# A decoder trunk on one core: where the dense pieces of a round stand, and how early casts and preparation are issued

## What is computed

```python
def reference(x, positions, ...):
    for i in range(DEPTH):
        p = x @ w_in                                   # attention, gate and r, k, v columns
        y_a = dsa_sparse_mqa(...)                      # top-64 keys of 256 for each query
        y_b = rwkv7_time_mix(pr, pk, v, pw, pa, pg, ...)
        g_a, g_b = jnp.split(jax.nn.sigmoid(p_gate + b_gate[i]), 2, axis=-1)
        x = layer_norm(alpha * x + (g_a * y_a + g_b * y_b) @ w_out[i], ...)
        x = layer_norm(alpha * x + conv_glu_ffn(x, w_up[i], ...), ...)

def step(state, inp):                                  # the recurrence, 16 heads of 64
    sa = jnp.einsum('bhvk,bhk->bhv', state, -kk_t)
    state = state * w_t[:, :, None, :] + sa[..., None] * b_t[:, :, None, :] \
            + v_t[..., None] * k_t[:, :, None, :]
    return state, jnp.einsum('bhvk,bhk->bhv', state, r_t)
```

## Time and profile before

| | us |
|---|---|
| median of 3 runs | 1269.19 (1268.2 to 1271.25) |
| the profiled execution's own time | 1277.04 |
| its span, first to last instruction | 1274.8 |
| PE busy in the span | 1160.5 (91%) |
| DVE busy | 785.9 (62%) |
| ACT busy | 537.2 (42%) |
| prologue and rounds, layer 0 (from the end of the scores to the last round's y) | 79.5 to 375.2 |
| the same, layer 1 | 712.1 to 1008.6 |

### The profile page before, as it was taken

One profiled execution on the slowest core, in us unless ns is written; L12 is line 12 of the kernel. 1 busy time (PEld: TensorE's weight loads), 2 busy tenths in 40 slices (PEclk: granted clock), 3 DMA queues, 4 the chain that ended last, 5 costly groups with the idle time before them and its releaser, 6 DMA issues.

```text
span 1274.8 us, 29251 instructions
## 1 busy us (share of the span) xinstructions
PE 1160.5 (91%) x12328; PEld 1042.2 (82%) x12328; DVE 785.9 (62%) x1436; ACT 537.2 (42%) x938; POOL 50.6 (4%) x56
## 2 busy tenths in 40 slices
PE   7996989898988899999999969898989898999997
PEld 7775878787878799998797758787878887999985
DVE  1338557675747777775522565667667577777745
ACT  2232445453534455654212424344545434556531
POOL 0000000000000100000000000000000001000000
PEclk9988999999999899999999978999999998999999
DMA  7422222222336365556464212212222464555561
GB/s 268 147 74 79 68 76 69 76 68 75 102 116 207 118 220 182 183 188 205 144 201 149 81 44 68 77 66 76 68 68 102 144 209 149 194 182 182 187 208 68
DMA packets 45353, 165.38 MB, mean 130 GB/s; under 512 B 5136, under 2 KB 5392, under 8 KB 44976
## 3 DMA queue, kind: packets, MB, share of 16 engines
q1 hardware_dynamic: 42576, 154.02, 36.3%
q0 software_dynamic: 1504, 7.47, 1.8%
q10 hardware_dynamic: 1152, 2.10, 0.5%
HBM read 160.42 MB, written 3.15 MB: 128 GB/s over the span
## 4 chain that ended last, share of the span: by engine, by line
PE 76%; DVE 17%; ACT 3%; issue 3%; DMA 1%; POOL 0%; DVEq 0%; SPq 0%; ACTq 0%
PE ps L722 18%; PE ps L723 16%; PE ps L724 16%; PE ps L869 8%; PE ps L697 5%; PE ps L1028 3%; DVE ring_r L1516 3%; DVE keep L1934 1%; PE ps L1070 1%; PE ps L881 1%; DVE small L1932 1%; PE ps L798 1%; PE ps L770 1%; ACT mid_hi L1192 1%; DMA ring<-stream_dram 1%
## 5 line engine op out<-in xcount | busy, mean ns | idle before, releaser
L722 PE MATMUL ps<-x_tok_r,mid_hi 128*128 128x256 f32 x448 | 138.6, 309 | 15.0 <-DVE ring_r L1516 15.0
L723 PE MATMUL ps<-xT_r,mid_hi 128*128 128x256 f32 x448 | 127.6, 285 | 0.0
L724 PE MATMUL ps<-x_tok_r,ring_r 128*128 128x256 f32 x448 | 127.4, 284 | 0.0
L722 PEld LDWEIGHTS ps<-x_tok_r,mid_hi 128*128 128x128 f32 x448 | 86.2, 192 | 25.3 <-issue 12.6
L697 PE MATMUL ps<-xT,ring 128*128 128x256 f32 x448 | 102.8, 388 | 0.0
L697 PEld LDWEIGHTS ps<-xT,ring 128*128 128x128 f32 x448 | 86.3, 195 | 13.8 <-issue 1.6
L1516 DVE TENSOR_TENSOR ring_r<-ring,mid_hi 128x1024 fp32r<-128x1024 f32 x64 | 77.9, 1219 | 25.0 <-ACT mid_hi L1192 25.0
L723 PEld LDWEIGHTS ps<-xT_r,mid_hi 128*128 128x128 f32 x448 | 86.7, 193 | 0.0
L724 PEld LDWEIGHTS ps<-x_tok_r,ring_r 128*128 128x128 f32 x448 | 86.5, 193 | 0.0
L1633 DVE COPY_PREDICATED X_Y<-masks,ps 128x256 f32<-128x256 uint32 x80 | 35.3, 441 | 66.0 <-PE ps L869 54.7
L1192 ACT CAST mid_hi<-ring 128x1024 fp32r<-128x1024 f32 x64 | 67.2, 1054 | 12.7 <-PE ps L724 12.7
(11 more groups left out here) (443 smaller groups left out, 3394.8 us busy)
## 6 DMA issues: line engine op xcount, KB each, us to landing
ring<-stream_dram SPq DMA_DIRECT2D x281, 512.0 KB, 3.4
lora_w<-lora_dram POOLq DMA_DIRECT2D x2, 1536.0 KB, 7.2
W_bt<-rpar_dram POOLq DMA_DIRECT2D x4, 512.0 KB, 4.5
kt_V<-rpar_dram POOLq DMA_DIRECT2D x4, 512.0 KB, 5.4
x_tok<-x_dram SPq DMA_DIRECT2D x2, 512.0 KB, 4.6
v_saved_dram<-vs_dC ACTq DMA_DIRECT2D x4, 256.0 KB, 3.9
x_tok<-x_dram SPq DMA_DIRECT2D x1, 1024.0 KB, 5.3
vf<-v_saved_dram ACTq DMA_DIRECT2D x4, 256.0 KB, 3.6
```

Of the source, the lines that this page charges most:

```text
L722: pe.matmul(dst, lh, rh, start=start, stop=False)
L723: pe.matmul(dst, lh, rl, start=False, stop=False)
L724: return pe.matmul(dst, ll, rh, start=False, stop=stop)
```

## The change

Every round still has its 16 pieces, and every task stays. What changes:

- **Gaps of the pieces.** Six in the levels, at gaps without a task: 0, 1, 5, 6, 9, 10 (first round: 5, 6, 7, 9, 10, 12). Ten in the chunk steps, which now have three gaps each, `fill(14 + 3c)` before Q, `15 + 3c` after Q and `16 + 3c` after y: all of 14 to 24 but 16.
- **Order of the pairs.** k, then r, then v, then the gates (`RKV_ORDER`); r ends in chunk step 0, v in chunk step 2. In the last round two gate pairs come before the two `oa` pairs.
- **Tasks.** The squares go from gap 13 to gap 12; `prep_rnx` from before Q1 to after y0.
- **ACT.** The cast of a chunk step stands ahead of the wait for Q, with a second call after it in steps 1 and 2; `resetY` is ahead of the wait for v.
- **DVE.** `att_norm` goes from the end of level 3 to ahead of it; the addition `Sa = S + own` (`chunk_t`) goes right behind Z; the subtractions follow the new casts; `prep_bk` goes from step 3 to step 2, ahead of `prep_v`.
- **Prologue.** On PE `prep_1` comes first, then two pieces, then `prep_ss` and `prep_v`; on DVE `prep_decay` and `prep_pend` come before `prep_ss`.

```diff
-LEVEL_GAPS = [list(range(4, 12))] + [[0, 1] + list(range(4, 10))] * (GROUPS - 1)
+LEVEL_GAPS = [[5, 6, 7, 9, 10, 12]] + [[0, 1, 5, 6, 9, 10]] * (GROUPS - 1)
+CHUNK_GAPS = [14, 15, 17, 18, 19, 20, 21, 22, 23, 24]
 OA_EARLY = 2
-GAPS = 14 + CHUNK_GAPS
+RKV_ORDER = (1, 0, 2)
+GAPS = 14 + 3 * NCH
...
+def gap_of(g, piece):
+    return (LEVEL_GAPS[g] + CHUNK_GAPS)[piece]
...
+def round_pairs(g):
     if g + 1 == GROUPS:
-        return [("oa", i) for i in range(OA_EARLY)]
-    return [("rkv", 3 * (g + 1) + 2)] + gates_of(g)
+        return gates_of(g) + [("oa", i) for i in range(OA_EARLY)]
+    return [("rkv", 3 * (g + 1) + t) for t in RKV_ORDER] + gates_of(g)
...
@@ PE, wkv @@
-                    fill(14 + 2 * c)
-                    if g + 1 < GROUPS and c == 1:
-                        prep_rnx(r + 1)
+                    fill(14 + 3 * c)
...
-                    fill(15 + 2 * c)
+                    fill(15 + 3 * c)
...
                     mm.then_inc(*pe_wkv.inc(r, f"y{c}"))
+                    if g + 1 < GROUPS and c == 0:
+                        prep_rnx(r + 1)
+                    fill(16 + 3 * c)
...
@@ PE, prologue @@
-                for k, p in enumerate((prep_ss, prep_1, prep_v, prep_rnT)):
-                    p(r0)
+                for k, ps_ in enumerate(([prep_1], [prep_ss, prep_v], [prep_rnT], [prep_rnx])):
+                    for p in ps_:
+                        p(r0)
                     for piece in first[2 * k:2 * k + 2]:
                         piece()
-                prep_rnx(r0)
...
                     if g + 1 < GROUPS:
-                        gaps[VALUES].append(lambda: prep_ss(r0 + g + 1))
+                        gaps[SQUARES].append(lambda: prep_ss(r0 + g + 1))
...
@@ ACT @@
             def chunk(r, c):
+                mids_up_to(r // GROUPS, mids_by(GAPS * (r % GROUPS) + 13 + 3 * c))
                 act.wait_ge(*pe_wkv(r, f"Q{c}"))
                 act.copy(Qs[:, :, :], step64(3)).then_inc(*act_wkv.inc(r, f"Q{c}"))
...
                         chunk(r, c)
-                        mids_up_to(l, mids_by(GAPS * g + 14 + 2 * c))
...
+                        if c in (1, 2):
+                            mids_up_to(l, mids_by(GAPS * g + 15 + 3 * c))
...
@@ DVE @@
-                prep_ss(r0)
                 prep_decay(r0)
                 prep_pend(r0)
+                prep_ss(r0)
                 topk(0)
...
                 prep_arc(r0)
+                prep_bk(r0)
                 prep_v(r0)
-                prep_bk(r0)
...
                     for lev in range(LEVELS):
+                        if lev == 3:
+                            att_norm(l, g)
                         if lev:
                             level(r, lev)
...
-                        if lev == 3:
-                            att_norm(l, g)
...
                             chunk_z(r, c)
+                            if c < NCH - 1:
+                                chunk_t(r, c)
+                            mids_up_to(l, mids_by(GAPS * g + 13 + 3 * c))
...
                             elif nxt and c == 2:
                                 prep_arc(r + 1)
+                                prep_bk(r + 1)
                             elif nxt:
                                 prep_v(r + 1)
-                                prep_bk(r + 1)
+                        else:
+                            mids_up_to(l, mids_by(GAPS * g + 13))
                         if c < NCH - 1:
                             chunk_s(r, c)
+                        if c in (1, 2):
+                            mids_up_to(l, mids_by(GAPS * g + 15 + 3 * c))
...
-                        mids_up_to(l, mids_by(GAPS * g + 13 + 2 * c))
```

More of the change, by code:

```diff
@@ L117, in gates_of, with pairs_done @@
     return [("gate", i) for i in range(start, start + GATES_CHUNKS[g])]
-def level_pairs(g):
-    return [("rkv", 3 * (g + 1)), ("rkv", 3 * (g + 1) + 1)] if g + 1 < GROUPS else gates_of(g)
-def chunk_gap(g, piece):
-    return piece * CHUNK_GAPS // max(4 * len(chunk_pairs(g)), CHUNK_GAPS)
-def pairs_done(g, c):
-    return [p for i, p in enumerate(chunk_pairs(g)) if chunk_gap(g, 4 * i + 3) // 2 == c]
+def pairs_done(g, lev=None, c=None):
+    ends = [(p, gap_of(g, 4 * i + 3)) for i, p in enumerate(round_pairs(g))]
+    if c is None:
+        return [p for p, n in ends if n < 14 and -(-(n - 3) // 2) == lev]
+    return [p for p, n in ends if n >= 14 and (n - 14) // 3 == c]
 def gate_slots(pairs):
@@ L155, in rkv_slots @@
 def rkv_slots(g):
-    return [("rkv", 8 * t + GB * g + b) for t in range(3) for b in range(GB)]
+    return [("rkv", 8 * t + GB * g + b) for t in (RKV_ORDER if g else range(3)) for b in range(GB)]
 SLOTS = [(l, *s) for l in range(DEPTH) for s in stream_order(l)]
@@ L509, in trunk @@
                                            + (["thv"] if r >= GROUPS else []) for r in range(R)])
-        dve_prep = Steps(sem("dve_prep"), [["ss", "s", "cum", "cp", "pend", "rnT", "kkn", "k2", "kb", "arc"]
-                                           + (["v1", "v2", "v"] if r >= GROUPS else [])
-                                           + ["bneg", "kp", "rkk"] for r in range(R)])
+        dve_prep = Steps(sem("dve_prep"), [(["ss"] if r % GROUPS else []) + ["s", "cum", "cp", "pend"]
+                                           + ([] if r % GROUPS else ["ss"]) + ["rnT", "kkn", "k2", "kb", "arc", "bneg", "kp"]
+                                           + (["v1", "v2", "v"] if r >= GROUPS else []) + ["rkk"] for r in range(R)])
         pool_prep = by_round("pool_prep", ["rn"])
@@ L1103, in _ @@
                 for g in range(GROUPS):
-                    gaps = {n: [] for n in range(14 + CHUNK_GAPS)}
-                    for n, p in enumerate(sum([pair_pieces(l, p, xT) for p in level_pairs(g)], [])):
-                        gaps[LEVEL_GAPS[g][n]].append(p)
-                    for n, p in enumerate(sum([pair_pieces(l, p, xT) for p in chunk_pairs(g)], [])):
-                        gaps[14 + chunk_gap(g, n)].append(p)
+                    gaps = {n: [] for n in range(GAPS)}
+                    for n, p in enumerate(sum([pair_pieces(l, p, xT) for p in round_pairs(g)], [])):
+                        gaps[gap_of(g, n)].append(p)
                     gaps[LOGITS].append(lambda: att_logits(l, g))
@@ L1195, in rkv @@
                 r = GROUPS * l + g
-                if t == 0 and g:
+                if t == RKV_ORDER[0] and g:
                     act.wait_ge(*dve_prep(r - 1, "rkk"))
@@ L1677, in chunk_s @@
                 if c:
-                    dve.tensor_tensor(Sa[:, :, :], S[:, (c + 1) % 2, :, :], own, ALU.add).then_inc(*dve_wkv.inc(r, f"T{c}"))
                     dve.wait_ge(*dve_wkv(r, f"T{c}"))
@@ L1985, in _ @@
                             bonus(r)
-                        for t in range(2):
-                            if nxt and level_before(g, t) == lev:
-                                rkv(l, g + 1, t)
-                        if lev == 3:
-                            att_norm(l, g)
+                        for kind, i in pairs_done(g, lev=lev):
+                            if kind == "rkv":
+                                rkv(l, g + 1, i % 3)
                         if not nxt and lev == 4:
```

40 lines of the change are left out of this document (17 added, 23 removed).

## The result

The kernel after takes 1236.78 us, the median of four executions (1234.7 to 1237.69); the kernel before took 1270.22 beside it (1268.2 to 1271.99). The ratio is 0.9735, interval 0.9714 to 0.9756. Predicted were 1236 and a range of 1221 to 1252. The profiled execution took 1237.3, its span is 1235.0.

The account below looks back on a forecast made before the run. PE, busy 1160.5 of 1274.8 us, bounds the kernel through idle and slow-clock time. Terms 8.9 + 7.9 + 2 x 9.1 + 1.4 - 3.6 = 32.8 us off the median 1269.2 give 1236, range 1221 to 1252.

Parts of the forecast that it names:

- Prologue, layer 0: Start of layer 0: prep_1 directly after the scores removes DVE's 8.29 us hole ahead of dA; gain 8.9 us.
- Layer 1: Prologue of layer 1: 5.9 us from the earlier start, 2.1 from prep_v behind b_k, less 0.1; gain 7.9 us.
- First rounds: First round of each layer: waits for the first mid cast and W shrink, one slow-clock stretch goes; gain 9.1 us each.
- Chunk steps: Chunk steps of each round: casts ahead of Q and pieces after y cover waits for ring_r and S; gain 1.8 us.
- the 0.5 us which the prediction named as a sign of being wrong: Chunk steps 1 to 3: PE waiting over 0.5 us for Zs or S would show the forecast wrong.
- Levels of the later rounds: Levels of later rounds: new waits of 4.0 us at XW0, y_back, bonus and level 3; loss of 1.2 us per round.
- goes, since it now runs while PE does bonus and level 3: Later rounds' levels: the 1.8 us wait for att_norm (scratch) vanishes through att_norm's earlier place on DVE.
- Clock: Later rounds: 4.5 slow-clock stretches of 2.4 us behind waits of 2.2 us, 10.9 against 7.3 before; loss of 3.6 us.
- The first: Chunk steps 1 and 3: DVE's full queue makes S or Zs late, 14 us lost, 1250 us; chance 0.15.
- The second: Levels of the later rounds: the holes do not open since W at XW0 is copied earlier, 1222 us; chance 0.11.
- the third: Prologue gives half: slow clock stays on the two pieces and PE sets the gram start, 1244 us; chance 0.10.
- The fourth: Slower than before: a late cast in chunk step 1 delays S1, Z2 and later steps, 1272 us or more; chance 0.03.

Follow-up runs that it names:

- the move of one piece: The kernel before with one piece of the later rounds moved from gap 8 to gap 10, att_norm left at the end of level 3: 1290.75 us (1.0124).
- undoing both halves: The kernel after with chunk-step casts behind the copy of Q on ACT and their subtractions behind S on DVE: 1243.9 us (0.9769).
- the version with the W copy first: The kernel after with y_square on ACT behind the copy of W0 of level 1 instead of ahead of it: 1219.71 us (0.9588).
- the best version: The kernel after with y_square behind the first W copy of level 1, prep_rnx back before Q1, and gap 17's piece at gap 16: 1209.72 us (0.9501).

## Why the prediction was right, and where it was wrong

Gram starts and the last sums of y divide the two profiled executions; their spans differ by 39.8 us, of which 17.9 are the prologues, 19.2 the first rounds, 0.0 the six later rounds and 2.7 what lies behind layer 1's rounds. The terms were 16.8, 18.2, -2.2 (1.4 less 3.6) and 0. The spans differ by some 6 us more than the medians (33.4), since the profiled execution of before lay that much over its median; the prediction took the sum off the median, and 32.8 met 33.4. That the two meet within 1 us is partly luck: the terms were read from the profiled execution, and against its 39.8 us they are 7.0 short, 1.1 in the prologues, 1.0 in the first rounds, 2.2 in the later rounds and 2.7 behind them. The 0.0 of the later rounds is itself a sum, 1.1 us gained in layer 0 and 1.1 lost in layer 1.

- **Prologue, layer 0: right.** 8.9 predicted. The gram start moved from 114.47 to 104.77; 0.58 of that was there before the part that changed, so 9.1. DVE sets the start, with PE idle for 2.02 us before it. **Layer 1:** 7.9, and 8.2 from the last sum of y of layer 0 on, which takes in the FFN. The prologue alone gave 18.9 on the chip, 2.1 over its terms, which is inside its interval. The slow stretch of 6.83 us at 80.99 is gone as well, as the forecast's full clock for the two pieces wanted it, but since DVE sets the gram start, nothing shows that it adds to the gain.
- **First rounds: right in sum, wrong in one cause.** 9.1 predicted each; they fell by 10.7 and 8.5. Of the 2.45 us wait in the last level I wrote "ACT being late behind the squares and the transposed probabilities", and that a piece and the squares at gap 12 cover it. In the move of one piece, ACT instead waits for DVE's shift of k, 2.14 us, and the trace of the first round of before shows the same chain:

```profile
152.77 0.83 DVE L1507 SCALAR_TENSOR_TENSOR rs_ks<-ps,cpar,rs_ks 128x255 f32<-128x255 f32 x2
```

```profile
153.64 0.91 ACT L1239 ACTIVATE tmp<-rs_ks,cpar 128x256 f32<-128x256 f32 x2 [2.15 <-DVE rs_ks L1507]
```

  In after k is done by gap 9 instead of 11 in a first round, ACT's `tmp` there begins at 131.71 without a wait, and PE has none for W. The order of the pairs, for which I had no term, so bears on it; the order and the work at gap 12 were not tried apart. The clock gave more than its term of 2.8 us: the prediction let the two stretches at the start of a first round stay, and PE's busy time in the first rounds fell by 4.2 and 2.8 us although each got a new stretch behind `prep_rnx` (147.90 and 762.30).
- **Chunk steps: right.** The waits for `ring_r` are gone, and those for S but for one of 0.56 us in each last round. That is over the 0.5 us which the prediction named as a sign of being wrong; it stood there before too, and the last rounds prepare no next one. 1.5 us was predicted for `ring_r`, as two waits; undoing both halves brings 1.46 back, as one wait at another place, so the size says less than it seems. `prep_rnx` waits 0.82 us where Z waited up to 0.6, for `ang`, the copy of rnT; 0.4 more was predicted. The sum of y waits 1.54 us instead of 1.03 in layer 1, the 0.5 that the prediction had for `prep_v`.
- **Levels of the later rounds: right in sizes.** Predicted and measured in us: XW0 2.2 and 2.23, `y_back` 0.5 and 0.40, bonus 0.9 and 0.93, XW0 of level 3 0.4 and 0.06. The step that failed is "goes, since it now runs while PE does bonus and level 3": the wait for `scratch` goes by the piece at gap 10, and `att_norm` may stay where it was. The sum did not notice, since the change does both.
- **Clock: right in kind, mixed in its terms.** The prediction had 4.5 stretches in the later rounds that cost 2.4 us each; there were seven, of 3.41 us at the lower clock, that cost some 1.5 each, and three of the seven do not stand at XW0 but behind `prep_rnx` (212.76, 827.15, 892.01), a place I had not named. What a stretch costs was close: the version with the W copy first has one in its second round, the window shown below, and PE is busy there for 57.42 us against 55.96 in the best version at full clock, 1.46 for 3.41 us, or 0.43 for each us; my row had said 0.40. The Trainium skill ("TensorE: Matmul & The Clock Gate", Terms) puts it at the throttled time times 1 - K/N, half of it here, which would be an estimate of 1.7 for such a stretch; the measured 1.46 decides. Seven cost about 10.2 against 10.9 predicted: more stretches than I had, each cheaper than I had it, and the two errors cancel.

```profile
166.53:227.40 60.87, 57.42 (x986) 51.13 (x986) 42.37 (x82) 28.93 (x63) 3.47 (x3) 0.97 0.23 76
```

- **Rivals.** The first (DVE's queue in steps 1 and 3) did not come true in the kernel after, but its mechanism is real and close: with the cast one hand-over later, DVE's S is late in six of eight rounds and 30 us go. The second fell with the holes at XW0, `y_back` and the bonus, the third with the gram start. The fourth had the first one's mechanism, and I gave it 0.03 since ACT is idle for more than half of a round. That argument was weak: ACT's idle time there is time spent waiting for PE in order, and it was an order, not a load, that cost the 30 us.

## What to carry to other kernels

Filling a hole with dense work moves it only if the chain behind it gets shorter. Of the 33 us, about half came from letting the operation that DVE waits for go first, and the levels gave nothing, since XW0 hung on one ACT copy queued behind squares that PE did not need yet; putting that copy first was worth another 17 us. So ask of each wait what stands ahead of its releaser in that engine's queue, before asking where the filler goes.

When a cast on one engine feeds a subtraction on another, an in-order wait couples everything behind both. Move such pairs together: with both halves late the loss was 7 us, with one half late it was 30.
